# Values of two attention stages multiplied as pairs of blocks with 512 moving columns

## Time and profile before

| | |
|---|---|
| median of 3 runs | 1967.04 us (1966.97 to 1967.35) |
| the profiled execution | 1967.15 us, its span 1965.4 us |
| busy: PE, DVE, ACT, POOL | 1951.8 us, 1039.3 us, 721.2 us, 28.1 us |
| granted TensorE clock | 1.0 (full, 2.4 GHz) in the mean |
| layer B, its first block to its last step | about 598 to 832 us |
| stage C, the same | about 1204 to 1462 us |

### The profile page before, as it was taken

One profiled execution on the slowest core, in us unless ns is written; L12 is line 12 of the kernel. 1 busy time (PEld: TensorE's weight loads), 2 busy tenths in 40 slices (PEclk: granted clock), 3 DMA queues, 4 the chain that ended last, 5 costly groups with the idle time before them and its releaser, 6 DMA issues.

```text
span 1965.4 us, 24706 instructions
## 1 busy us (share of the span) xinstructions
PE 1951.8 (99%) x9684; PEld 1592.0 (81%) x9684; DVE 1039.3 (53%) x1461; ACT 721.2 (37%) x1058; POOL 28.1 (1%) x64
## 2 busy tenths in 40 slices
PE   9999999999999999999999999999999999999998
PEld 7877888888888777778888888777778998888886
DVE  6354665435555444575524556776545575533443
ACT  5443432212343344442212233455433462312322
POOL 0100000000000000000000000000000000000001
PEclk9999999999999999999999999999999999999999
DMA  4421333333233222233243323321333423333322
GB/s 155 99 66 57 114 84 87 96 106 98 70 101 129 86 86 70 81 86 103 74 115 94 99 78 108 107 65 59 98 86 86 129 65 91 112 108 86 86 85 86
DMA packets 283248, 181.33 MB, mean 92 GB/s; under 512 B 19083, under 2 KB 273140, under 8 KB 283164
## 3 DMA queue, kind: packets, MB, share of 16 engines
q1 hardware_dynamic: 272223, 179.43, 31.1%
q10 hardware_dynamic: 10941, 0.75, 0.4%
HBM read 176.33 MB, written 2.75 MB: 91 GB/s over the span
## 4 chain that ended last, share of the span: by engine, by line
PE 96%; DVE 2%; ACT 1%; issue 0%; DMA 0%; DVEq 0%; ACTq 0%
PE psum L1982 30%; PE psum L1984 29%; PE psum L1983 29%; PE psum L2216 1%; PE psum L2270 1%; DVE wl L1270 1%; PE psum L2225 1%; PE psum L2187 1%; PE psum L2243 1%; PE psum L2321 1%; PE psum L2283 1%; PE psum L2154 1%; PE psum L2291 1%; ACT wh L718 0%; PE psum L2598 0%
## 5 line engine op out<-in xcount | busy, mean ns | idle before, releaser
L1270 DVE TENSOR_TENSOR wl<-stage,wh 128x2048 fp32r<-128x2048 f32 (+2 forms) x164 | 349.8, 2133 | 164.8 <-ACT wh L718 161.4
L718 ACT CAST wh<-stage 128x2048 fp32r<-128x2048 f32 (+2 forms) x158 | 280.4, 1774 | 240.6 <-PE psum L1984 238.3
L1982 PE MATMUL psum<-xl,wh 128*128 128x512 f32 (+1 forms) x768 | 302.3, 394 | 1.0 <-DVE wl L1936 0.5
L1982 PE MATMUL psum<-x2l,wh 128*128 128x512 f32 x768 | 301.7, 393 | 1.0 <-DVE wl L1270 0.6
L1984 PE MATMUL psum<-x2h,wh 128*128 128x512 f32 x768 | 299.0, 389 | 0.0
L1983 PE MATMUL psum<-x2h,wl 128*128 128x512 f32 x768 | 298.9, 389 | 0.0
L1984 PE MATMUL psum<-xh,wh 128*128 128x512 f32 (+1 forms) x768 | 292.8, 381 | 0.0
L1983 PE MATMUL psum<-xh,wl 128*128 128x512 f32 (+1 forms) x768 | 292.6, 381 | 0.0
L756 ACT ACTIVATE work<-work 128x512 f32<-128x512 f32 x66 | 41.7, 632 | 389.3 <-DVE work L1361 389.3
L1982 PEld LDWEIGHTS psum<-xl,wh 128*128 128x128 f32 x768 | 144.4, 188 | 40.3 <-issue 11.1
L1982 PEld LDWEIGHTS psum<-x2l,wh 128*128 128x128 f32 x768 | 144.1, 188 | 34.1 <-issue 1.5
(11 more groups left out here) (399 smaller groups left out, 2808.4 us busy)
## 6 DMA issues: line engine op xcount, KB each, us to landing
stage<-in_ffn_w_gate_dram SPq DMA_DIRECT2D x44, 512.0 KB, 4.0
stage<-in_ffn_w_up_dram SPq DMA_DIRECT2D x44, 512.0 KB, 5.3
stage<-in_w_in_dram SPq DMA_DIRECT2D x40, 512.0 KB, 4.1
stage<-in_ffn_w_down_dram SPq DMA_DIRECT2D x32, 384.0 KB, 3.9
stage<-in_a_w_in_dram SPq DMA_DIRECT2D x22, 512.0 KB, 4.8
stage<-in_w_gate_dram SPq DMA_DIRECT2D x22, 512.0 KB, 4.0
stage<-in_w_up_dram SPq DMA_DIRECT2D x22, 512.0 KB, 5.3
stage<-in_ffn_w_down_dram SPq DMA_DIRECT2D x32, 320.0 KB, 3.7
```

The costliest lines, as they stand in the source:

```text
L718: nc.scalar.copy(wh[:, par, 0:n], stage[:, par, 0:n]).then_inc(w_hi, 1)
L1270: vec.tensor_tensor(wl[:, par, 0:n], stage[:, par, 0:n], wh[:, par, 0:n].bitcast(F32), ALU.subtract).then_inc(w_lo, 1)
L1982: mm(out, a_hi, b_lo, start=start, stop=False)
```

## The change

In layer B the blocks `B_v0` and `B_v1` become the wide pair `B_w0`, in stage C the blocks `C_va0` and `C_va1` become the wide pair `C_wa`. Both are multiplied as a whole ahead of step 0, in banks 4 to 7. The streams lose 32 units (B) and 16 (C), and their rates are new: B has 5 in each of the 32 steps, C has 6 in steps 0 to 15, 5 in 16 to 23, 6 in 24 to 31. `C_v` blocks remain for the neighbourhood heads, `B_v2` and `B_v3` for the later heads of layer B. The transposes of the norms in stage C go to bank 0 and stand between the two halves of the pair. PE waits for `rst_ready` in B before the pair (its third token tile is written over the transposed norms), and in both stages for the evictions of the pair before step 0. `place_values` waits for the scores of step 15.

```diff
             add("B_q0", "copy", 1)
+            add("B_w0", "wide", 2)
             for i in range(4):
-                add(f"B_v{i}", "tokens", 1)
+                if i >= 2:
+                    add(f"B_v{i}", "tokens", 1)
...
-                add(f"C_v{c}", "tokens", 1)
+                if c == "a0":
+                    add("C_wa", "wide", 2)
+                if c[0] == "b":
+                    add(f"C_v{c}", "tokens", 1)
...
-B_RATE = [8] * 6 + [6] * 12 + [5] * 14 + [9] * 2
+B_RATE = [5] * 32 + [8] * 2
...
-C_RATE = [6] * 24 + [7] * 8 + [4] * 2
+C_RATE = [6] * 16 + [5] * 8 + [6] * 8 + [4] * 2
...
-        TURN_BANK = {1: 6, 2: 4}
+        WIDE = ("A_w1", "A_w2", "A_w3", "B_w0", "C_wa")
+        TURN_BANK = {1: 6, 2: 0}
...
                 sp.wait_ge(block_out, b + 1)
+                sp.wait_ge(s_done, C_SCORE0 + 2 * DA_STEPS)
...
@@ scalar, layer B and stage C
+                split_of(first + 3)
+                split_of(first + 4)
...
+                split_of(first + 4)
@@ vector, wide_out and its calls
+                layer = "ABC".index(s.name[0])
+                bank = 4 + 2 * i if layer else 2 * ((s.b0 + i) % 2)
...
+                if layer == 2:
+                    dve.wait_ge(c_lo, 2)
+                    vec.tensor_tensor(cva[:, t, :], ps, rst[:, t, 0:1].to_broadcast([P, 2, 512]), ALU.mult
+                                      ).then_inc(block_out, 1)
+                    return
+                if layer == 1:
+                    vec.tensor_tensor(bv[:, 0:4, t, :].rearrange("p c t n -> p t c n"),
...
+                split_of(first + 3)
+                split_of(first + 4)
+                wide_out(st["B_w0"], 0)
+                wide_out(st["B_w0"], 1)
...
-                epilogue_of(first + 2)
+                split_of(first + 4)
+                wide_out(st["C_wa"], 0)
+                wide_out(st["C_wa"], 1)
@@ tensor, layer B
                 turn_rs(1)
+                pe.wait_ge(rst_ready, 2)
+                wide_block("B_w0", 0)
+                wide_block("B_w0", 1)
                 units_of(b_stream, 0, 0, 2)
+                pe.wait_ge(block_out, first + 4)
@@ tensor, stage C
                 multiply("C_ka0", first + 1, 1, False)
-                multiply("C_va0", first + 2, 0, False, 6)
+                pe.wait_ge(norm_root, 4)
+                wide_block("C_wa", 0)
+                pe.wait_ge(block_out, first + 1)
                 turn_rs(2)
+                wide_block("C_wa", 1)
+                units_of(c_stream, 0, 0, 3)
+                pe.wait_ge(block_out, first + 4)
                 pe.wait_ge(rst_ready, 3)
```

More of the change, by code:

```diff
@@ L217, in build @@
     blocks = [s for s in st.values() for _ in range(s.blocks)]
-    b_names = [n for n in st if n[:2] == "B_" and n not in ("B_k0", "B_q0", "B_outB")]
+    b_names = [n for n in st if n[:2] == "B_" and n not in ("B_k0", "B_q0", "B_w0", "B_outB")]
     a_names = [n for n in st if n[:2] == "A_" and n not in ("A_q0", "A_k0", "A_v0", "A_outB")]
-    c_names = [f"C_{q}{c}" for c in ("a1", "b0", "b1") for q in "qkv"] + ["C_ga"]
+    c_names = ["C_qa1", "C_ka1"] + [f"C_{q}{c}" for c in ("b0", "b1") for q in "qkv"] + ["C_ga"]
     with ExitStack() as ctx:
@@ L512, in sources @@
                     r = DT // 2 * P * i
-                    w = a_w_in[0][r:r + DT // 2 * P, :]
-                    return [cols(w, n + 256 * int(name[3]), 256) for n in (1024, 2048)], (DT // 2, 256)
+                    w, c = {"A": (a_w_in[0], (1024, 2048)), "B": (w_kv, (D, D + 256)),
+                            "C": (w_in[0], (1024, 1280))}[name[0]]
+                    c = [n + (256 * int(name[3]) if name[0] == "A" else 0) for n in c]
+                    return [cols(w[r:r + DT // 2 * P, :], n, 256) for n in c], (DT // 2, 256)
                 if name[:3] in ("B_k", "B_q", "B_v"):
@@ L610, in load_stage @@
                 s = st[name]
-                if s.blocks == 1 or s.kind == "rows":
+                if s.blocks == 1 or s.kind in ("rows", "wide"):
                     if name == "down20":
@@ L642, in _ @@
                         load_one(s, s.name, i)
[L643 removed]
+                elif name == "B_k1":
                     load_b_stream()
@@ L1308, in epilogue @@
                 s = st[name]
-                bank = 6 if name == "C_va0" else 2 * par
+                bank = 2 * par
                 ps = psum[:, bank:bank + 2, :]
@@ L1387, in wide_out @@
                 else:
-                    dve.wait_ge(wide_done, c)
-                dve.wait_ge(rst_ready, 1)
+                    dve.wait_ge(wide_done, WIDE.index(s.name) + 1)
+                dve.wait_ge(rst_ready, 1 + layer)
                 t, ps = slice(2 * i, 2 * i + 2), psum[:, bank:bank + 2, :]
+                if layer == 2:
[5 more added lines that the diff above has]
+                    vec.tensor_tensor(bv[:, 0:4, t, :].rearrange("p c t n -> p t c n"),
+                                      ps.rearrange("p t (c n) -> p t c n", n=P),
+                                      rst[:, t, 0:1].unsqueeze(2).to_broadcast([P, 2, 4, P]), ALU.mult
+                                      ).then_inc(block_out, 1)
+                    return
+                c = int(s.name[3])
                 for dst, src in ((av[:, 2 * c:2 * c + 2, t, 0:P], ps[:, :, 0:256]),
@@ L2066, in unit @@
                     pe.wait_ge(w_lo, b + 1)
-                if u == 0 and not (wide and i):
+                if u == 0 and not wide or u == i == 0 and s.name[0] == "A":
                     pe.wait_ge(block_out, b - 1)
-                if u == 8 and wide and i == 0:
+                if u == 8 and wide and i == 0 and s.name[0] == "A":
                     pe.wait_ge(block_out, b)
@@ L2075, in unit @@
                     k, token = 4 * i + kk, slice(t * P, (t + 1) * P)
-                    last = three(psum[:, (2 * (s.b0 % 2) + t) % 4, :], inh[:, k, token], inl[:, k, token],
+                    bank = (2 * (s.b0 % 2) + t) % 4 if s.name[0] == "A" else 4 + t
+                    last = three(psum[:, bank, :], inh[:, k, token], inl[:, k, token],
                                  whp[:, kk * 512:(kk + 1) * 512], wlp[:, kk * 512:(kk + 1) * 512], k == 0, k == DT - 1)
@@ L2098, in unit, with wide_block @@
                     last.then_inc(mm_done, 1)
+            def wide_block(name, i):
+                for u in range(st[name].units):
+                    unit(st[name], i, u)
             def units_of(stream, step, i, of):
@@ L2277, in attention_c @@
                         if head < DA_HEADS:
-                            pe.wait_ge(block_out, st[f"C_va{head // 2}"].b0 + 1)
+                            pe.wait_ge(block_out, first + 4)
                         else:
```

16 lines of the change are left out of this document (5 added, 11 removed).

## The result

The changed kernel took 1972.85 us in the median of 7 runs (1971.88 to 1975.00), the kernel before 1967.11 us (7 runs, 1966.94 to 1967.44): a ratio of 1.0030, 95% interval 1.0021 to 1.0040. It is slower by 5.7 us. I had forecast 1971.0 us. The profiled execution took 1974.13 us, its span is 1972.4 us. Of all runs reported here one is left out of the comparison, a slow one of experiment 3 with 3258.87 us, at a granted clock of 0.556 in the mean.

The account below looks back on a forecast made before the run. PE was taken as the bound, busy for 99% of the span. The terms -0.9 + 0 + 0.1 + 4.4 + 0.2 gave +3.8 to +3.9 us on 1967.04 us, so 1971.0 us, with a wide range of 1967.5 to 1974.0.

Parts of the forecast that it names:

- Part 1: Matmuls of both moved pairs: 96 of 512 columns replace 192 of 256, -1.25 us per stage, -2.5 us in all.
- Part 2: Start of layer B: PE waits for ACT's copy of the norms, +0.34 us; layer B in all -0.9 us.
- Part 3: Layer B's steps with five units: the softmax chain still fits, 0 us, upper bound 1.5 us.
- Part 4: Start of stage C: PE waits 2.4 us for second-half weights, three old waits go; +0.1 us net, matmul gain included.
- Part 5: Stage C: C_qb1 ends in step 15, its eviction holds DVE; PE waits 2.7 and 1.7 us, +4.4 us.
- Part 6: Placing the values in stage C, behind step 23's maxima on SP's queue: +0.2 us, bounds 0 and 1 us.
- The sum: All parts together: +3.8 to +3.9 us on the median of 1967.04 us, giving 1971.0 us.
- rival *(c): A new wait of 2.4 or 2.7 us in stage C drops PE's clock once: +2.5 us, 1973.5 us; chance 0.07.
- the sign I had named myself: Forecast is wrong if the granted clock is below 1.0 between 1238 and 1370 us.
- the forecast's own range: Range of the main forecast for the whole kernel: 1969.5 to 1972.5 us; chance 0.62.
- rival *(b): Stage C's delay spreads: a further step or the second placing pays 1 to 3 us more, 1973 us; chance 0.18.
- Rival *(a): The sixth block of stage C's stream doesn't hold DVE: -0.6 us, 1966.4 us; chance 0.13.

Follow-up runs that it names:

- experiment 3: Only the lines of the change that name layer B, put into the kernel before: 1966.41 us, ratio 0.9997.
- Experiment 8: Changed kernel with the edits of 4 and Experiment 6, each 512-column matmul of the moved pairs issued as two of 256: 1967.63 us, +1.65 us against both edits.
- Experiment 1: Changed kernel with stage C's unit counts altered, five units in steps 10 to 16, so that C_qb1 ends in step 17: 1970.51 us.
- Experiment 6: Changed kernel with five units in step 15 and six in step 16, so that C_qb1 ends in step 16: 1969.69 us.
- experiment 9: Stage C's part of the change alone, layer B as in the kernel before: 1974.72 us, ratio 1.0038 to the kernel before.
- 4: Changed kernel with the split of block first + 3 ahead of the second key's casts at stage C's start: 1970.05 us.
- experiment 5: Changed kernel measured once more, unaltered: 1972.95 us, ratio 1.0031 to the kernel before.
- experiment 2: Changed kernel with PE's two long waits in stage C filled by 10 and 12 matmuls whose result nobody reads: 1971.49 us.
- experiment 11: Kernel of experiments 10 with DVE's split of step 17 put at the end of that step: 1975.93 us, +2.1 us.
- experiments 10: Changed kernel with the edits of 4 and Experiment 6, and layer B's norms transposed between the pair's halves: 1973.82 us.

## Why the prediction was right or wrong, point by point

**Part 1 (the matmuls), right.** Experiment 8 has 1.23 us a pair in the traces (0.8 us in the medians), part 1 had 1.25.

**Part 2 (start of layer B), right but for 0.2 us.** The idle time at the pair was 0.28 us, and the pair's start moved by 0.36 us (23.18 us behind the first matmul of `B_k0` and not 22.82), where part 2 had 0.34. From there to the first scores it took 23.37 us, as part 2 has it. Layer B gained 0.68 us in the ledger and 0.59 us alone, not 0.9. What the rest is no run shows.

**Part 3 (five units a step in layer B), right:** no wait. Experiment 1 showed that this does not carry over to the steps 10 to 16 of stage C.

**Part 4 (start of stage C), right in mechanism and size, but for the clock.** The wait was 2.33 us (2.4 said), and without a fall the way from PE's restart to the transposes 0 took 18.78 us, where the part has 1259.6 - 1240.87 = 18.73 us. With the fall it was 1.54 us more.

**Part 5 (`C_qb1` in step 15), right.** The product ended at X + 9.06 us (X + 9.05 said), the transposes 16 stood at X + 13.21 (X + 13.0), the wait was 2.75 us (2.7). The second wait of 1.7 us was 0.98 + 0.35 = 1.33 us without a fall. Experiment 1 took the hold away and with it both waits. Experiment 6 shortened it to 2.69 us and moved it by a step, which left nothing of the first wait and 0.57 + 0.35 us of the second.

**Part 6 (placing), right in kind:** 0.37 and 0.21 us where 0.2 stood.

**The sum and the clock.** An execution without falls took 1971.31 us, 4.36 us over the median of before beside it, where the sum had 3.8 to 3.9: +5.04 us in stage C for the 4.7 us of parts 4 to 6, and -0.68 us in layer B for -0.9 us. The step that failed is the weight of rival *(c)*. I gave it 0.07 and one fall. By the sign I had named myself, a granted clock below 1.0 between 1238 and 1370 us, the prediction was wrong there in the first profile. The measured 1972.85 us lie outside the forecast's own range (1969.5 to 1972.5), and they lie in the wide one only because that was stretched for rival *(b)*, which did not come: that it held them is luck. The profiled executions with the long waits of stage C have nine such waits (2.26 to 2.75 us), and six of them have a fall behind them: two each in the first profile and in experiment 9, one each in 1 and 4, none in 5 and 6. So the median, 5.7 us over the kernel before, is the forecast with falls on top of it in part of the runs, not one case or the other. My argument against, "before, no wait behind the start is over 1 us, and the clock held", was true and no evidence: it said nothing of waits of 2.3 us and more, which I had just forecast. The rule of the Trainium skill that I named there (the page "TensorE: Matmul & The Clock Gate", Part 1, the clock gate: idleness puts the array back to 1.2 GHz) is borne out by the first profile and by experiment 2; that the same waits in experiment 5 had no fall behind them, the rule as I told it doesn't say, and no run here shows what decides it. Rival *(b)*, a third step paying, did not come: behind the transposes 17 only the placing shows a bracket. Rival *(a)* is out by DVE's idle 7.05 us.

## What to carry to other kernels

When a block drops out of a stream of fixed rates, recount in which step each later block ends: its eviction may meet a wait that never had to be waited for, and the 1.25 us that a pair of blocks gains here is less than one such wait. Before moving work on one engine, read what stands behind the moved instruction on every in-order queue that serves it; both of my own late edits failed there (5.81 us and 2.50 us) and once the queues were put in order they gave 0.75 us together in the median. Price a new wait on TensorE as long as these (2.3 us and more) at its length and a fall of the clock behind it in part of the executions.

## What the runs showed of the hardware that I had not expected

The clock's fall behind a wait is not certain: with waits of 2.28 and 2.75 us it stayed at 1.0 in one execution of the same kernel and fell to 0.5 twice, for 3.41 us each, in another; behind the 2.50 us of experiment 11 it stayed at 1.0. Behind waits of 1.69 us and less it did not fall in any profile here, and at one of 5.81 us it stood at half for 6.83 us in both profiles that have it (experiments 10 and 11), from before the restart on. A kernel with such waits also shows it in its times: 2.9 us between the fastest and the slowest of 8 runs, against 1.25 us in 11 when the waits were filled. And a slow clock costs less than its matmuls say where the engine would have waited anyway: 1.54 us where no wait followed, 0.78 us where one of 0.98 us did.
